# A transformer program on one core: another order for its head and for the seam into the mixer

## What is computed

```python
mod = silu(c) @ w_ada + b_ada            # 9 vectors of 1024
sh1, sc1, g1, sh2, sc2, g2, sh3, sc3, g3 = split(mod, 9)
u = rmsnorm(h, norm_ffn1) * (1 + sc1) + sh1
h = h + 0.5 * g1 * swiglu(u, w_ffn1_up, w_ffn1_down)
u = rmsnorm(h, norm_mix) * (1 + sc2) + sh2
h = h + g2 * hybrid_mixer(u, w_in, ...)  # projections, convolutions, gated delta rule
u = rmsnorm(h, norm_ffn2) * (1 + sc3) + sh3
h = rmsnorm(h + 0.5 * g3 * swiglu(u, w_ffn2_up, w_ffn2_down), norm_final)
```

## Time and profile before

| | |
|---|---|
| median of three runs | 1462.38 µs (1461.26 to 1464.34) |
| profiled execution, its span | 1462.3 µs |
| TensorE busy | 1381.9 µs (95%) |
| DVE, ACT, GpSimd busy | 907.1, 713.0, 726.6 µs |
| DMA | 258.19 MB, mean 177 GB/s |
| chain that ended last | TensorE 79%, DVE 13%, ACT 4% |

### The profile page before, as it was taken

How to read it: one execution, slowest core, us unless ns; L and a number is a source line. 1 busy time by engine, 2 the same in 40 slices (tenths; PEclk the granted TensorE clock), 3 DMA queues, 4 the chain that set the end, 5 groups by cost and what they waited for, 6 DMA issues and landing times.

```text
span 1462.3 us, 28264 instructions
## 1 busy us (share of the span) xinstructions
PE 1381.9 (95%) x11769; PEld 1246.5 (85%) x11769; DVE 907.1 (62%) x1348; ACT 713.0 (49%) x1143; POOL 726.6 (50%) x805
## 2 busy tenths in 40 slices
PE   6999998999999898999999899789999999999998
PEld 3788886798988888978888789778899999888998
DVE  3788634676978347577555577666643585676533
ACT  1655532665545333445555545545543466555442
POOL 0677653332333223556656444346665544566653
PEclk8999999899999999999999999999999999999999
DMA  8888687653333443467555643445556544455651
GB/s 308 297 271 262 222 301 253 147 156 117 101 104 120 143 146 99 159 205 231 190 181 183 209 144 116 134 126 174 187 192 198 173 127 134 152 188 182 200 189 42
DMA packets 234445, 258.19 MB, mean 177 GB/s; under 512 B 8457, under 2 KB 211663, under 8 KB 234319
## 3 DMA queue, kind: packets, MB, share of 16 engines
q1 hardware_dynamic: 230272, 252.35, 52.8%
q10 hardware_dynamic: 4047, 4.04, 1.4%
HBM read 253.75 MB, written 2.62 MB: 175 GB/s over the span
## 4 chain that ended last, share of the span: by engine, by line
PE 79%; DVE 13%; ACT 4%; issue 2%; DMA 1%; DVEq 0%; SPq 0%; ACTq 0%
PE ps L696 34%; PE ps L690 22%; PE ps L692 11%; DVE w_lo L1899 3%; PE ps L942 2%; PE ps L657 1%; ACT w_hi L1302 1%; DVE arow L1924 1%; PE ps L669 1%; PE ps L986 1%; DVE mt L2149 1%; DMA raw<-in_w_ada 1%; DVE sil L2149 1%; PE ps L731 1%; DVE sil L1999 1%
## 5 line engine op out<-in xcount | busy, mean ns | idle before, releaser
L639 POOL TENSOR_TENSOR w_lo<-raw,w_hi 128x256 fp32r<-128x256 f32 x800 | 726.1, 939 | 718.5 <-ACT w_hi L1302 718.5
L1302 ACT CAST w_hi<-raw 128x1024 fp32r<-128x1024 f32 (+1 forms) x408 | 411.4, 1045 | 191.3 <-PE ps L696 113.1
L690 PE MATMUL ps<-u_hl,w_hi 128*128 128x512 f32 x1216 | 427.8, 396 | 8.7 <-DVE w_lo L1899 4.7
L1899 DVE TENSOR_TENSOR w_lo<-raw,w_hi 128x1024 fp32r<-128x1024 f32 x204 | 276.3, 1355 | 137.3 <-ACT w_hi L1302 135.7
L696 PE MATMUL ps<-u_hl,w_hi 128*128 128x256 f32 x1856 | 351.1, 290 | 7.5 <-DVE yaf L2129 2.7
L692 PE MATMUL ps<-u_hl,w_lo 128*128 128x256 f32 x1216 | 339.6, 279 | 0.0
L696 PEld LDWEIGHTS ps<-u_hl,w_hi 128*128 128x128 f32 x1856 | 292.5, 194 | 17.8 <-issue 8.1
L690 PEld LDWEIGHTS ps<-u_hl,w_hi 128*128 128x128 f32 x1216 | 227.9, 187 | 65.7 <-issue 13.3
L696 PE MATMUL ps<-u_hl,w_lo 128*128 128x256 f32 x928 | 264.1, 285 | 0.0
L692 PEld LDWEIGHTS ps<-u_hl,w_lo 128*128 128x128 f32 x1216 | 229.3, 189 | 0.3 <-issue 0.2
L696 PE MATMUL ps<-mid_hl,w_hi 128*128 128x256 f32 x1024 | 182.6, 282 | 0.0
(11 more groups left out here) (370 smaller groups left out, 1564.5 us busy)
## 6 DMA issues: line engine op xcount, KB each, us to landing
raw<-in_mlp_w SPq DMA_DIRECT2D x64, 1024.0 KB, 5.2
raw<-in_w_ffn_up SPq DMA_DIRECT2D x44, 1024.0 KB, 5.0
raw<-in_w_ada SPq DMA_DIRECT2D x36, 1024.0 KB, 6.3
raw<-in_w_in SPq DMA_DIRECT2D x30, 1024.0 KB, 5.1
raw<-in_w_ffn_down SPq DMA_DIRECT2D x16, 1024.0 KB, 5.3
raw<-in_attn_w_in SPq DMA_DIRECT2D x12, 1024.0 KB, 5.0
raw<-in_mlstm_w_in SPq DMA_DIRECT2D x12, 1024.0 KB, 5.1
raw<-in_w_ffn_down SPq DMA_DIRECT2D x8, 768.0 KB, 4.6
```

Of the source, the lines that this page charges most:

```text
L639: pool.tensor_tensor(w_lo[half][:, kt, :], src[:, kt, :], w_hi[half][:, kt, :].bitcast(F32), ALU.subtract).then_inc(low_ready(n, h)[0], 1)
L690: pe.matmul(two(b - 10 + m), x, z, start=(first and kt == ks.start), stop=False, skip_group_check=True)
L1302: act.copy(w_hi[t % HALVES][:, 0:k, :], src).then_inc(hi_ready, 1)
L1899: dve.tensor_tensor(w_lo[half][:, 0:k, :], src, w_hi[half][:, 0:k, :].bitcast(F32), sub)\
```

## The change

It has four parts.

1. **Loads and plan in the head.** Part 1 is split: its first half is loaded before slab 0, its second half after it. The sums of part 1 get a bank of their own.
2. **Order in the head.** TensorE transposes the parameters and takes the column sums of part 2 ahead of the squares. Parts 0 and the first half of part 1 follow. `first_slab` runs the first half of slab 0, then the second half of part 1 and its column sums, then the other half of slab 0. ACT and DVE take part 1 between tiles 3 and 4 of the activations. The four dummy products go.
3. **Order at the seam.** F1 is loaded ahead of part 13. The squares of tiles 6 and 7 stand between the two halves of part 12. ACT computes the root first, then copies the row of part 12, then rounds F1. One dummy product instead of two. Part 13 is summed after F0, `spread` stands half a slab later.
4. **GpSimd.** `BY_POOL` names F1: both its halves are worked by GpSimd.

```diff
-    for p in (0, 1):
-        plan.ada(p, False)
-        plan.group("mod", p)
+    plan.ada(0, False)
+    plan.group("mod", 0)
+    plan.ada(1, False, halves=(0,))
+    plan.due = [("ada", 3)]
+    plan.group("mod", 1)
...
-    plan.ada(13)
-    plan.group("mod", 13)
     for kind, key in FIRST + FILL:
+        if (kind, key) == FIRST[1]:
+            plan.ada(13)
+            plan.group("mod", 13)
...
-BY_POOL = ()
+BY_POOL = (FIRST[1],)
...
+            def first_slab(ready):
+
+                n = plan.slab[("f1", 0, 0)]
+                b = open_bank("f1", 0, 0)
+                half(n, 0, b, U, True, False, ready)
+                ada_sums(1, (1,))
+                mod_sums(1)
+                half(n, 1, b, U, False, True, ready)
...
-                    if g in downs:
+                        ada_sums(downs[g], (0,))
+                        squares(then, (6, 7))
+                        ada_sums(downs[g], (1,))
+                    elif g in downs:
                         ada_sums(downs[g])
-                if then not in LATE:
-                    squares(then, (6, 7))
...
             ada_sums(3)
-            squares("ffn1")
             pe.wait_ge(s("params_in"), 16 * NPAR)
...
             mod_sums(2)
+            squares("ffn1")
             mod_sums(3)
+            ada_sums(0)
...
-            for p in range(2):
-                ada_sums(p)
-                mod_sums(p)
+            mod_sums(0)
+            ada_sums(1, (0,))
...
                     next(pieces)
+                    if i == 1:
+                        ada_sums(13)
                     if i == 3:
                         gates()
-                    if i == 5:
+                    if i == 6:
                         spread(0)
...
-            warm(4)
             ffn("f1", "ffn1", "mix")
-            ada_sums(13)
-            warm(2)
+            warm(1)
             mixer()
...
+                if name == "mix":
+                    row_out(12)
+                    split_hi(plan.slab[FIRST[1]], 0)
                 shifted(name)
                 if name == "mix":
-                    row_out(13)
+                    split_hi(plan.slab[FIRST[1]], 1)
...
                 for k in range(KD):
+                    if name == "ffn1" and k == 4:
+                        row_out(1)
+                        split_hi(0, 1)
...
-                ahead(plan.slab[FIRST[0] if name == "mix" else ("f2", 0, 0)])
+                if name == "ffn2":
+                    ahead(plan.slab[("f2", 0, 0)])
                 root(name)
```

More of the change, by code:

```diff
@@ L289 @@
 PAIRED = ("f1", "f1d", "f2", "f2d", "m0", "m1")
-APART = (4, 5, 6, 7, 8, 9, 10, 11, 12, 13, 16, 17)
+APART = (1, 4, 5, 6, 7, 8, 9, 10, 11, 12, 13, 16, 17)
 def turn(p):
@@ L534, in by_pool @@
         def by_pool(n):
-            return n <= LAST and plan.key[n][0] in BY_POOL
+            return n <= LAST and plan.key[n] in BY_POOL
         by_vector = [n for n in range(len(plan.slabs)) if not by_pool(n)]
@@ L545, in low_ready @@
             if by_pool(n):
-                return s("lo_ready_pool"), by_gpsimd.index(n) + 1
+                return s("lo_ready_pool"), 4 * by_gpsimd.index(n) + 4
             return s("lo_ready0"), by_vector.index(n) + 1
@@ L743, in ffn @@
                     for t in range(2):
-                        slab((name, i, t), (name, i, t), U, ready=ready if i == 0 else None)
+                        if (name, i, t) == ("f1", 0, 0):
+                            first_slab(ready)
+                        else:
+                            slab((name, i, t), (name, i, t), U, ready=ready if i == 0 else None)
                     if i - 2 in ups:
@@ L1402, in ffn @@
                             fresh(then, (name + "d", g - 1), g - 1)
[L1403 to L1407, removed]
                 if then in LATE:
@@ L1448, in _ @@
             act.activation(rms, bank(2)[:, 0:S], ACT.Sqrt, scale=1.0 / D, bias=cc[:, 0:1]).then_inc(s("rms_ready"), 1)
+            row_out(0)
             act.wait_ge(s("brow_ps"), 1)
             link(act.copy(brow, bank(6)[0:8, 0:384]))
-            row_out(0)
-            row_out(1)
-            ahead(-1)
+            split_hi(0, 0)
             follow = Follow(act, s)
@@ L1538, in mixer @@
                         act.dma_start(bias_dram, brow[:, None, :].broadcast_to([8, P, 384])).then_inc(s("brow_out"), 16)
+                    if i == 2:
+                        row_out(13)
                     if i == 3:
@@ L2031, in ffn @@
                     for k in range(KD):
+                        if k == 4:
+                            mod_out(1)
                         shifted_low(norm_name, k)
@@ L2098, in _ @@
             mod_out(0)
-            mod_out(1)
             ahead(-1)
```

## The result

The changed kernel takes 1479.33 us (median of four runs, 1478.8 to 1480.5), the kernel before beside it 1461.82 (four runs). The ratio is 1.0114, with an interval of 1.0098 to 1.0131: slower by 17.5 us, where 11.8 us of gain were forecast. The profiled execution has a span of 1478.7 us against 1462.3, that is +16.4.

A forecast was written before the change was run, and what follows sets the result against it. TensorE was taken as the bound, busy 1381.9 of 1462.3 us, with time to win only at its idle, dummy or slow-clock places. Head -3.1 and seam -8.7 gave 1462.3 - 3.1 - 8.7 = 1450.5 us, range 1445.5 to 1457.

The forecast's parts named there:

- The loads allow this: Head: slab 0's load lands at about 28 us; later loads may slip DVE's row work but do not delay TensorE.
- is there long before: Seam: F1 takes the place of a load issued at 236.09 us, so its weights arrive well before they are needed.
- a new wait of 0.8: Seam, behind F2: F3's `w_lo` comes 6.6 us behind the gate products while F2 takes 5.75, so TensorE waits 0.8 us.
- Forecast -3.1 us: Head: slab 1 ends at 50.4 us instead of 53.5, a gain of 3.1 us.
- a bound of +0.5: Head's worst end: shift 0 at 32.7 us and the first half slab at half clock, 2.8 us more, lose 0.5 us.
- T + 4.6: Head: half of slab 0 takes 2.8 us from T + 1.9, where T is when shift 0 is there, taken as 31.9 us.
- The rival with the lower clock: Head and seam: fewer dummy products and remaining pauses keep TensorE at half clock, +20.0 us, giving 1469.6 us; chance 0.05.
- Reciprocal 6.7 us earlier: Seam: with F1 loaded early and the root first, DVE's reciprocal starts at 248.0 instead of 254.70 us.
- The disturbance by GpSimd: Seam, F0: GpSimd's work on F1 slows DVE's scaling, costing 2.3 us, so F0 ends at 259.9 us.
- Gate products -6.7: Seam: part 13 behind F0 ends at 261.8 instead of 268.5 us, and the lead holds through the gate products.
- Gate sums -9.6: Seam: the 2.02 us wait ahead of `spread` goes and `spread` takes 1.8 instead of 3.52 us, raising the lead from 5.9.
- The rival in which DVE and ACT become the bound: Mixer's first slabs: DVE and ACT set the pace, so the seam gives only 4.9 us, total 1454.3 us; chance 0.14.

The follow-up runs named there:

- late write: The changed kernel with the 1.5 MB write of the bias rows issued after the 15th mixer piece instead of the second: 1465.68 us, ratio 1.0024.
- small write: The changed kernel with bias rows written in 32 instead of 128 copies (384 KB), read back in four transfers: 1458.3 us, ratio 0.9975.
- early write: The kernel before with only the bias write moved, to the start of the mixer, ahead of F3's load: 1468.96 us, ratio 1.0054.
- half write: The changed kernel with the bias rows written in 64 copies (768 KB) and two read-backs: 1467.55 us, ratio 1.0027.
- head part alone: The kernel before with only the change's first two parts (loads and order in the head): 1464.0 us, ratio 1.0012.
- seam part with the small write: The kernel before with only the change's seam and GpSimd parts, bias rows written in 32 copies (384 KB): 1455.38 us, ratio 0.9951.

## Why the prediction was wrong

**The step that failed is the time at which F3's weights are there.** "The loads allow this" was worked out for the head, up to slab 3. At the seam the prediction followed F1 alone ("is there long before"). It took F3 as loaded and counted only DVE's share: `w_lo` ready 6.6 us behind the gate products, a new wait of 0.8. The load itself and the write of the bias rows were put at nothing, without a reason. Measured: F3's `w_lo` is ready 23.7 us behind the gate products (295.65 + 1.23 against 273.16), and the wait is 18.5 us. Both facts were there to be read: the write of 1.5 MB stands in ACT's program behind the second mixer piece, and F1's new place gives F3 a buffer that comes free only behind GpSimd's second half. Together they turned the order of load and write around. The experiments show it three ways: the write moved or shrunk removes the wait (late write, small write), the write moved forward alone makes a wait in the kernel before (early write), and half the write makes a third of the wait (half write).

**The head: steps right, the clock wrong.** Forecast -3.1 us, with a bound of +0.5; measured +2.5 in the profiled execution, and for the head part alone a ratio of 1.0012, which is no gain. The step is "T + 4.6", half a slab at full clock. It took 5.4 us (34.16 to 39.6) instead of 2.8, since each pair of products took 0.64 us instead of 0.35, and the second half began slow as well. The rival with the lower clock had this mechanism, but was given 0.05, and its argument against ("the clock came back within about ten microseconds under thinner work") took for granted that the pauses inside slab 0 weigh no more than the thin work there. With the pauses filled the same steps give 49.97 to 51.12 us, against a forecast of 50.4. The gain of 3.1 us was too large even so: its other end, 53.5 us, is one execution, and against the mean of the unchanged head, 52.0, the filled head (50.7 in the mean) gains 1.3.

**The seam up to the wait: right.** Reciprocal 6.7 us earlier, measured 6.6. The disturbance by GpSimd was put at 2.3 us; with F1 on DVE the stretch is 1.6 us shorter. Gate products -6.7 and measured -6.8. Gate sums -9.6, and in the small write -9.3 with a head that is within 0.2 us of the kernel before. The rival in which DVE and ACT become the bound showed in small part at most. In the seam part with the small write TensorE waits 1.6 us for ACT at 311.67 us, ahead of the delta rule, where the kernel before has no such wait; in the late write it is 0.5 us, and in the small write nothing.

**What the range lacked.** Of the 16.4 us, 12.9 stand at the gate sums. By the seam's own steps (-9.4 from the small write), the head and the wait they come to 2.5 + 18.5 - 9.4 = 11.6; the remaining 1.3 fit the granted clock of 0.50 that the changed kernel has from 290 to 300 us, behind the wait. Another 3.0 us come between 906 and 1161 us of the kernel before, in the attention stage, where the waits are the same and the clock stands lower in places (0.89 from 958 to 974 us, against 1.00 in the same stretch of work before). The prediction said that a microsecond won at the seam should stay won. The small write keeps 3.9 of its 9.3 us to the end, the seam part with the small write all of its 9.8. Executions of one kernel spread by 8.6 us in the small write (1453.2 to 1461.8) and by 12.0 in the late write, so this is no property of the change that one profile could show. Why the clock falls in one execution and not in the other stays open.

Without the write's collision the change would have been faster, as forecast, but not by as much: the small write measures 1458.3 us, still above the range's 1457, where 1450.5 was forecast. The seam part gives -6.9 us where -8.7 was forecast, and with the head's pauses filled the whole change gives -8.0 (1454.3 us) where -11.8 was forecast.

## What to carry to other kernels

When a change moves a load, list every transfer of every queue near its new place, the slow stores and small-packet writes of other engines too, and ask on which side of them the load now stands. A write that costs nothing today may be hidden only because the next loads are already on their way. And where a step puts dense products earlier but with pauses between them, price it at the lower clock until a run shows otherwise, or fill the pauses.

## What the runs showed of the hardware

**A write from few partitions holds half of the DMA engines.** The write comes from 8 partitions and takes a steady 45% of the 16 engines, which is 7.1 engines, for about 30 us. The Trainium skill, page "DMA: Bandwidth & Descriptors", section on why a DMA increments its semaphore by 16, says that a copy is spread over the largest number of engines up to 16 that divides the slowest dimension of both of its sides; 8 here gives 8 engines, and the trace agrees. Its packets are slow: 0.446 x 16 x 10 us over 329 packets is 0.22 us for each 1.5 KB, while a packet of a load takes 0.05 us for 1.0 KB (0.175 x 160 / 569).

**A load behind it moves one half at once and waits with the other.** The changed kernel's DMA view from 264 to 270 us, the first microseconds of F3's load:

```profile
q10 hardware_dynamic: 200, 0.31, 44.9%
q1 hardware_dynamic: 520, 0.52, 27.2%
```

Half of the load's 1 MB is there by 270 us. That this is the half of the free engines is an inference from the amount. From 274 to 278 us the loads moved nothing, while the write moved 133 packets; from 280 to 290 us both moved 321. The Trainium skill, page "DMA: Bandwidth & Descriptors", section on queues, rings and completion order, says that an engine takes turns between its queues by packets, and means by a packet a group of descriptors that is drained before the engine changes. Turns agree with the equal counts from 280 to 290 us. No run here shows the size of such a group, or why the loads' other half stood still before.

**DVE beside GpSimd takes twice as long.** Elementwise operations with two inputs in SBUF took 0.94 to 0.95 us while GpSimd worked, and 0.47 behind it. With F1 on DVE they took 0.48 throughout. The prediction had this from the head; the seam shows it without the doubt of an average.

**With pauses in the head the clock stayed low, with dummy products in them it did not.** In the head of the changed kernel each half of slab 0 follows a pause (1.47 and 1.75 us) and runs almost whole at 1.2 GHz, though TensorE has no idle time inside it. In the late write and the head alone the clock was 1.00 from 20 to 28 us, and 0.50 from 32 to 36 us around a pause of 2.81 us. All five profiled executions of the changed head without dummy products had such slow stretches; the three with the five dummy products held 2.4 GHz from 28 to 52 us. It is no rule for every place: at the seam of the changed kernel pauses of 0.71, 1.05 and 0.70 us stand in a stretch with a granted clock of 1.00 (250 to 260 us), and in the late write the same stretch has 0.68.
